# Scan mixer: VectorE's first recurrence part is units 0 to 2, GpSimd has units 3 and 4, and tiles 3 to 5 are gathered ahead of the last tile's write

## The reference, cut to what matters

```python
def _s5_direction(u, lam_re, lam_im, log_dt, b_re, b_im, c_re, c_im, reverse):
    ...
    lam_bar = jnp.exp(lam * dt)
    bu = lax.complex(jnp.einsum('bsgp,gnp->bsgn', u, b_bar.real), jnp.einsum('bsgp,gnp->bsgn', u, b_bar.imag))
    _, hs = lax.associative_scan(combine, (a, bu), axis=1, reverse=reverse)   # h = lam_bar * h_before + bu
    return jnp.einsum('gpn,bsgn->bsgp', c, hs).real

def s5_mixer(h, ...):
    y = (y_fwd + y_bwd).reshape(b, s, d) + d_skip.astype(jnp.float32) * hf
    g = jax.nn.gelu(y).astype(h.dtype)
    val, gate = jnp.split(g @ w_glu, 2, axis=-1)
    return val * jax.nn.sigmoid(gate)
```

## Time and profile before

| what | us |
|---|---|
| median of 3 runs | 2922.12 |
| the runs | 2919.21 to 2925.47 |
| the profiled execution, its own time | 2919.29 |
| its span in the profile | 2917.5 |
| TensorE busy | 2792.2 (96% of the span) |
| VectorE, ScalarE, GpSimd busy | 1572.0, 1135.4, 341.0 |

### The profile page before, as it was taken

How to read it: one execution, slowest core, us unless ns; L and a number is a source line. 1 busy time by engine, 2 the same in 40 slices (tenths; PEclk the granted TensorE clock), 3 DMA queues, 4 the chain that set the end, 5 groups by cost and what they waited for, 6 DMA issues and landing times.

```text
span 2917.5 us, 38672 instructions
## 1 busy us (share of the span) xinstructions
PE 2792.2 (96%) x15536; PEld 2274.7 (78%) x15536; DVE 1572.0 (54%) x2342; ACT 1135.4 (39%) x1792; POOL 341.0 (12%) x426
## 2 busy tenths in 40 slices
PE   9999999599999999999999899999999999999887
PEld 8788888488888877777788588888988888776665
DVE  7876664755434434554535654344644344754656
ACT  5332232264212324646647342123432123543443
POOL 0333222710000001111112300000000000110100
PEclk9999999799999999999999799999999999999989
DMA  4245558453444223222222322222122222211101
GB/s 142 97 149 169 156 153 248 170 173 109 130 130 122 88 80 108 70 91 80 91 91 91 130 99 100 101 101 99 61 101 100 94 95 101 83 52 37 57 16 46
DMA packets 116020, 307.08 MB, mean 105 GB/s; under 512 B 28176, under 2 KB 73808, under 8 KB 87296
## 3 DMA queue, kind: packets, MB, share of 16 engines
q1 hardware_dynamic: 108064, 278.39, 29.0%
q10 hardware_dynamic: 6336, 21.76, 2.1%
q0 software_dynamic: 1440, 4.46, 0.5%
HBM read 266.91 MB, written 41.85 MB: 106 GB/s over the span
## 4 chain that ended last, share of the span: by engine, by line
PE 84%; DVE 6%; ACT 4%; POOL 3%; issue 3%; DMA 1%; ACTq 0%; SPq 0%; DVEq 0%; POOLq 0%
PE ps L94 82%; PE ps L99 2%; POOL s_ L121 1%; ACT wh_ L117 1%; DVE wl_ L121 1%; POOL H_ L121 1%; ACT hh_ L117 1%; DVE s5wn_ L121 0%; DVE R_ L121 0%; ACT R_ L117 0%; DMA raw_<-in_w 0%; ACT Pm_ L116 0%; ACT sq_ L117 0%; DMA yb_<-yx 0%; POOL s5G_ L139 0%
## 5 line engine op out<-in xcount | busy, mean ns | idle before, releaser
L94 PE MATMUL ps<-hh_,wh_ 128*128 128x512 f32 x2184 | 867.8, 397 | 4.5 <-DVE hl_ L121 3.3
L94 PE MATMUL ps<-hl_,wh_ 128*128 128x512 f32 x2184 | 854.0, 391 | 0.0
L94 PE MATMUL ps<-hh_,wl_ 128*128 128x512 f32 x2184 | 853.5, 391 | 0.0
L121 DVE TENSOR_TENSOR wl_<-raw_,wh_ 128x2048 fp32r<-128x2048 f32 (+4 forms) x245 | 483.2, 1976 | 506.3 <-ACT wh_ L117 505.8
L117 ACT ACTIVATE wh_<-raw_ 128x2048 fp32r<-128x2048 f32 (+3 forms) x244 | 400.7, 1649 | 352.4 <-PE ps L94 330.1
L94 PEld LDWEIGHTS ps<-hh_,wh_ 128*128 128x128 f32 x2184 | 412.3, 189 | 102.8 <-issue 9.4
L94 PEld LDWEIGHTS ps<-hh_,wl_ 128*128 128x128 f32 x2184 | 412.2, 189 | 87.4
L94 PEld LDWEIGHTS ps<-hl_,wh_ 128*128 128x128 f32 x2184 | 412.7, 189 | 86.5 <-issue 2.9
L94 PE MATMUL ps<-ah_,wh_ 128*128 128x512 f32 x704 | 275.1, 391 | 0.0
L94 PE MATMUL ps<-al_,wh_ 128*128 128x512 f32 x704 | 274.0, 389 | 0.0
L94 PE MATMUL ps<-ah_,wl_ 128*128 128x512 f32 x704 | 274.0, 389 | 0.0
(11 more groups left out here) (363 smaller groups left out, 3580.6 us busy)
## 6 DMA issues: line engine op xcount, KB each, us to landing
raw_<-in_w SPq DMA_DIRECT2D x203, 1024.0 KB, 4.9
sO<-s5ce_ SPq DMA_DIRECT2D x32, 256.0 KB, 3.8
sW<-s5wt_ SPq DMA_DIRECT2D x16, 512.0 KB, 6.1
sA<-os_ SPq DMA_DIRECT2D x24, 256.0 KB, 2.1
ol_<-sA SPq DMA_DIRECT2D x24, 256.0 KB, 3.9
sT<-sK SPq DMA_DIRECT2D x32, 128.0 KB, 4.1
wh_<-sO ACTq DMA_DIRECT2D x4, 1024.0 KB, 6.3
wl_<-sO ACTq DMA_DIRECT2D x4, 1024.0 KB, 7.5
```

The costliest lines, as they stand in the source:

```text
L94: return self.e.matmul(out, lhsT, rhs, start=start, stop=stop, skip_group_check=True)
L121: return Nothing() if self.e is None else self.e.tensor_tensor(out, a, b, op)
```

## The change

VectorE's first part becomes groups 0 to 23 (units 0 to 2) and GpSimd's becomes groups 24 to 39 (units 3 and 4). VectorE begins when unit 2 is in `H`, GpSimd when unit 4 is. `LEAD` goes from 18 to 28. Both halves of `hf` of units 0 to 2 are made by ScalarE; GpSimd makes the imaginary half of units 3 to 7. The steps of part 2 that are left are done 7, 5, 5, 5 and 6 at a time before the additions of units 0 to 4. SyncE issues the gather of tiles 3 to 5 before the write of tile 7.

```diff
-LEAD = 18
-PARTS = ((0, 16), (16, 24), (40, 24))
+LEAD = 28
+PARTS = ((24, 16), (0, 24), (40, 24))
 def part_of(un):
-    return 0 if un < 2 else 1 if un < 5 else 2
+    return 1 if un < 3 else 0 if un < 5 else 2
...
-        if ri:
+        if ri and un > 2:
             e.cp(o, h).then_inc(*e.up())
...
         state_copies(K, ac, un, 0)
+        if un < 3:
+            state_copies(K, ac, un, 1)
...
-        far = 128 * (at[1] - at[2]) - 48
+        far = 128 * (at[1] - at[2]) - 80
...
-    last[1] = K.at("out", "ch", 4, 1)
+    last[1] = K.at("out", "ch", 2, 1)
...
-        if un < 4:
-            for _ in range(7 if un == 0 else 5):
+        if un < 5:
+            for _ in range((7, 5, 5, 5, 6)[un]):
                 if at[2] < 64:
                     step(2)
-        if un == 4:
+        if un == 5:
             dv.mark("out", "s.work")
...
-    po.wait_ge(*K.at("out", "ch", 1, 1))
+    po.wait_ge(*K.at("out", "ch", 4, 1))
...
-    for un in range(8):
+    for un in range(3, 8):
         state_copies(K, po, un, 1)
...
+    spread(K, sp, 1, "U", range(8))
     staged_sync(K, sp, 7)
-    spread(K, sp, 1, "U", range(8))
     spread(K, sp, 2, "U", range(8))
```

## The result

The changed kernel takes 2930.18 us (median of 17 runs, 2920.93 to 2938.5) against 2921.43 (17 runs, 2917.81 to 2929.52). The ratio is 1.0028 with a 95% interval of 1.0018 to 1.0038: slower by 0.28%, some 8 us. The profiled execution took 2933.34, its span is 2931.4.

A forecast was written before the change was run, and what follows sets the result against it. The mixer's end was taken to follow unit 5's copies, held by VectorE's part 2: 595.8 against 594.24, +1.6. Added to the median forecast of 2922.1 this gave 2923.7 us, range 2918 to 2929.

The forecast's parts named there:

- VectorE's start: First recurrence step of VectorE's part 1: at 510.0 instead of 516.95, 7 us earlier.
- Gathers: SyncE's eight gathers of tiles 3 to 5: issued by 487.7 to 492.9; tile 7's write lands 3.9 us after issue.
- my two bounds for the last tiles: Landing of the gather of tiles 6 and 7: between 506.3 and 509.0, against 510.77 before.
- a landing after 512: Sign on SyncE's gathers: if they land after 512, the prediction is wrong.
- floor of 0.34 us an issue: SyncE's gather issues: none can take less than a single issue's 0.34 us.
- The slow rival: Late gathers delay tile 7's write and tiles 6 and 7; VectorE's start counts in full: +5.9, 2928.0, chance 0.09.
- From the start to unit 5: VectorE's way from its start to the end of part 2, where unit 5's copies begin: 85.8 us.
- the gap ahead of unit 2: TensorE waits for unit 2's four copies, 4.8 us against 3.6 of matmuls: a gap of 1.3 us.
- The second hole: TensorE, ready for unit 5 at about 593, waits for its copies: a gap of 4 to 6 us.
- Part 2 as the bound: VectorE's part 2 ends at 595.8, later than GpSimd's 594.2 demands, and sets the start of unit 5's copies.
- The head start: TensorE resumes with unit 0 at about 570.5, 6.2 us earlier, all spent in a new hole ahead of unit 5.
- The lock: GpSimd in its new place meets no VectorE scaling, so the shared ports do not hold it; otherwise +2.3 us.

The follow-up runs named there:

- e4: Changed kernel with tile 7's write issued by ScalarE instead of SyncE; 2921.67 us, ratio 1.0006 to the kernel before.
- e1: Changed kernel with SyncE issuing tile 7's write ahead of the gather of tiles 3 to 5 again; 2924.18 us, ratio 1.0010.
- e6: Changed kernel with SyncE issuing tile 7's write before the gather of tiles 3 to 5, and part 2's steps 13, 5, 5, 5, 0; 2920.83 us.
- e7: Changed kernel with the table transfers of units 6 and 7 moved behind unit 0's copies; 2934.03 us (four runs), ratio 1.0049.
- e5: Changed kernel with tile 7's write issued by ScalarE and part 2's steps 13, 5, 5, 5, 0; 2917.62 us, ratio 0.9996.
- e8: Changed kernel with tile 7's write by ScalarE, `LEAD` 24 and part 2's steps 13, 5, 5, 1; 2917.94 us, ratio 0.9986 to the kernel before.
- e9: The kernel of e5 measured again on a different chip; 2919.76 us, ratio 0.9992 to the kernel before.
- e2: Kernel before the change with only the gather of tiles 3 to 5 moved ahead of tile 7's write; 2919.75 us, ratio 0.9995.
- e3: Changed kernel with part 2's remaining steps done 13, 5, 5, 5, 0 at a time instead of 7, 5, 5, 5, 6; 2926.10 us, ratio 1.0015.

## Why the prediction was wrong

I forecast 2923.7, a shift of +1.6; the measured one is +8.2. For unit 5's copies the sum is: +1.6 forecast, VectorE's start 8.0 us later than forecast against the norm's matmul, the way from there to unit 5 1.3 us shorter, together the +8.3 of the table.

- **Gathers: the step that failed.** I had the eight gathers issued by 492.9 at the latest, at 0.98 us each, and tile 7's write landing 3.9 us after its issue. They were done at 495.7 (10.18 / 8 = 1.27 each), and the write took 9.2. The 0.98 was a mean over two gathers that do not cost the same. Before, the eight of tiles 3 to 5 took (496.78 - 490.62) / 8 = 0.77 us each and the smaller ones of tiles 6 and 7 took 1.18. In the changed kernel it was the other way round, 1.27 and 3.96 / 8 = 0.50. So it is not the size that set the price, but the place. At the new place the gathers are issued right behind 2.5 MB of tables and weights (`wh_`, `wl_` and `sW`, from 484.3 on). That these are what holds them is likely but was not tested by itself. The 3.9 came from a write that had no gathers in flight. Each was a price of the old place in the order, used for the new one.
- **What that made of the last tiles.** Against my 509.0, the later of my two bounds for the last tiles, the write was issued 2.8 us later and took 5.3 longer, the eight gathers behind it were issued 3.5 us faster, and the last of them landed in 7.7 instead of 5.4: 7 us, so 516.1. The prediction had named a landing after 512 as a sign that it was wrong. Its floor of 0.34 us an issue is not one either, since single issues took 0.30 in e4. SyncE's timeline before, the first gather of tiles 6 and 7:

```profile
496.78 2.30 SPq L161 DMA_DIRECT2D U_<-hx  x1
```

- **Why it is late.** Two causes add up. The write stands behind eight gathers in SyncE's queue (issued 495.7 instead of 490.2; by ScalarE at 490.0 in e4). And it shares the DMA engines: it took 3.6 and 3.9 us in e1 and e6 with nothing gathered ahead of it, 5.2 in e7 behind gathers but without the tables of units 6 and 7, 6.9 to 7.4 from ScalarE's queue with both (e4, e5, e8, e9), and 8.3 to 9.4 behind the gathers with both (changed, e2, e3). Before, this landing lay behind the gather of tiles 3 to 5; now it is in series with it. The Trainium skill, "DMA: Bandwidth & Descriptors", on queues, rings and completion order, says that SyncE's and ScalarE's queues are rings on the same 16 engines, which take them in turn. The trace agrees: changing the queue took away the place in line (issue at 490.0), but not the slow landing (7.2 us in e4).
- **The slow rival** had the right place and the right way for the cost (the start counted through to unit 5), and too small a chance, 0.09. I argued against it that the same bytes are moved and that the gather begins earlier. I had counted the landing of tile 7 in series, but at a price from where it was covered; how slow it would be at its new place, the bytes did not say.
- **From the start to unit 5** I had 85.8 us; 84.5 and 85.1 were measured. The steps of 0.77 and 0.97, GpSimd's 1.05 and the four copies in a row on ScalarE came as computed, and the gap ahead of unit 2 was 1.06 instead of 1.3.
- **The second hole** was forecast at 4 to 6 us and found at 5.55. The slower outputs of unit 5 behind it (6.13 us at a mean granted clock of 0.58) were covered, as I had said: from unit 5's first copy to the last stall it is 34.9 us, against 34.3 before.
- **Part 2 as the bound** was right for the changed kernel, as e3 shows. With about the start that I had forecast (e4) it was GpSimd's path that bound. Unit 0's outputs were there at 574.60 instead of 577.2 (5.46 us where I had 6.7), so VectorE's own work would have ended at 574.6 + 18.6 = 593.2, and unit 3's outputs came at 590.4 instead of 589.0 (5.38 us where I had 3.74). That six steps were left behind unit 3 is a choice of the change that costs 5 us of its own. My numbers leave VectorE 577.2 - 565.6 - 7 x 0.772 = 6.2 us idle ahead of unit 0's addition (5.25 measured), and I did not ask what else could stand there.
- **The head start** of 6.2 us never came in the changed kernel; in e4, where it came, it was spent ahead of unit 5 (4.3 us), as forecast, and ahead of unit 3 (2.0 us), which was not.
- **The lock.** GpSimd's first instructions in the changed kernel:

```profile
516.54 0.94 POOL L121 TENSOR_TENSOR s_<-H_,l_ 128x64 f32<-128x64 f32 x1 [21.41 <-ACT H_ L117]
517.56 0.58 POOL L121 TENSOR_TENSOR s_<-s_,H_ 128x32 f32<-128x32 f32 x1
...
583.57 0.25 POOL L121 TENSOR_TENSOR H_<-s_ 128x32 f32<-128x32 f32 x1
```

The late scaling (516.08 to 518.03) fell on GpSimd's start and held it for some 0.9 us, which I had excluded for its new place; in e1, where the scaling ended at 511.1, the first instruction took 0.32. The exclusive lock of the shared ports in the Trainium skill, "SBUF — State Buffer", on contention, is what both rows look like. It decided nothing here.

## What to carry to other kernels

A DMA that something later waits for has two prices: its place in the queue and its landing beside what is in flight; when it is moved behind others, neither can be taken from its old place, and a landing that was hidden before must be added to the chain. When a part's start is brought forward, ask first which arrival sets the new start, and then which fixed order of instructions eats the gain at the other end: here six steps, placed ahead of unit 0's addition instead of unit 4's, were worth some 4 to 5 us, about as much as the late transfer. The same late transfer cost nothing that could be measured in one partition and 4 us or more in the other, so an edit of the order and an edit of the parts have to be timed apart.

## What the runs showed that I had not expected

The granted clock makes the same work of TensorE cost different times. Unit 3's outputs took 5.38 us at a mean granted clock of 0.67 in e4 and e5, after TensorE had idled 2.0 and 2.2 us, and 3.75 at 1.00 in e8 and e9, where it had hardly idled; a gap of 1.06 ahead of unit 2 left the clock at 1.00. Unit 0's outputs, which begin at the low level (1.2 GHz) behind the long hole, took 5.4 to 6.7 us. So 1 to 2 us of a shift inside the mixer can depend on where the clock's changes fall, and not on the change.
